# Expert tiles in pairs: two experts of 32 rows in four column quarters of the array, and a routing without the gain row and the GpSimd products

## What is computed

```python
def hier_moe(h, w_rg, b_rg, w_re, b_re, w_gate, w_up, w_down):
    g_logits = hf @ w_rg + b_rg                        # 4 groups
    g_idx = argmax(g_logits)
    e_in = (hf @ w_re + b_re)[the 8 experts of g_idx]
    top_v, top_i = lax.top_k(e_in, 2)
    combine = softmax weight of the group x softmax of top_v
    out = sum over experts: (silu(x @ w_gate) * (x @ w_up) * combine) @ w_down
x = x + hier_moe(rmsnorm_2(x, ffn_norm), ...)
```

## Time and the profile before

| | us |
|---|---|
| median of 3 runs | 1720.14 (1718.44 to 1720.27) |
| the profiled execution's own time | 1715.29 |
| its span, first to last instruction | 1713.6 |
| mean granted TensorE clock over the span | 0.983 |
| PE busy, PEld busy | 1629.1, 1308.2 |
| DVE, ACT, POOL busy | 938.9, 786.5, 193.6 |
| chain that ended last, share of PE | 82% |

### The profile page before, as it was taken

The page is one execution under the profiler, slowest core; times in us unless marked ns, Lnnn a source line. Parts: engine busy times, 40 slices in busy tenths (PEclk is TensorE's granted clock), DMA queues, the critical chain, the costliest instruction groups (busy, mean ns, idle before and its releaser), DMA issues.

```text
span 1713.6 us, 22648 instructions
## 1 busy us (share of the span) xinstructions
PE 1629.1 (95%) x9347; PEld 1308.2 (76%) x9347; DVE 938.9 (55%) x1347; ACT 786.5 (46%) x1261; POOL 193.6 (11%) x241
## 2 busy tenths in 40 slices
PE   7999999999999999988999989899999994999998
PEld 6888888788887888876788879879989884555554
DVE  5454677654565454577645465887858656111112
ACT  6434544543456444476644445557746531112121
POOL 0000000100010000011100010500001003343441
PEclk9999999999999999999999999999999995999999
DMA  7454555455565455531555544424432375999993
GB/s 283 174 195 174 194 185 192 164 189 180 192 222 206 181 192 177 195 124 70 189 174 195 175 154 172 148 74 167 164 136 101 151 302 203 347 410 403 407 408 152
DMA packets 58455, 347.94 MB, mean 203 GB/s; under 512 B 13629, under 2 KB 13917, under 8 KB 18129
## 3 DMA queue, kind: packets, MB, share of 16 engines
q1 hardware_dynamic: 47520, 334.02, 52.7%
q0 software_dynamic: 10832, 12.48, 2.3%
HBM read 372.57 MB, written 13.89 MB: 226 GB/s over the span
## 4 chain that ended last, share of the span: by engine, by line
PE 82%; DVE 9%; ACT 3%; issue 2%; DMA 2%; POOL 1%; SPq 0%; DVEq 0%; ACTq 0%; POOLq 0%
PE A L397 30%; PE Y L427 19%; PE A L2946 8%; PE A L350 5%; PE A L335 4%; PE Y L2964 4%; DVE wlo L295 2%; PE A L411 1%; PE Y L366 1%; ACT whi L290 1%; DMA raw<-stream 1%; PE A L694 1%; PE A L2937 1%; DVE xn L494 1%; DVE h L495 1%
## 5 line engine op out<-in xcount | busy, mean ns | idle before, releaser
L295 DVE TENSOR_TENSOR wlo<-raw,whi 128x2048 fp32r<-128x2048 f32 (+1 forms) x227 | 499.2, 2206 | 241.8 <-ACT whi L290 241.3
L290 ACT ACTIVATE whi<-raw 128x2048 fp32r<-128x2048 f32 (+1 forms) x227 | 417.7, 1847 | 89.9 <-DMA raw<-stream 89.6
L397 PE MATMUL A<-whi,xh 128*128 128x512 f32 x768 | 310.0, 404 | 5.3 <-DVE wlo L295 5.3
L397 PE MATMUL A<-wlo,xh 128*128 128x512 f32 x768 | 302.4, 394 | 0.0
L397 PE MATMUL A<-whi,xl 128*128 128x512 f32 x768 | 300.7, 391 | 0.0
L397 PEld LDWEIGHTS A<-whi,xh 128*128 128x128 f32 x768 | 145.0, 189 | 35.3 <-DVE wlo L295 6.1
L397 PEld LDWEIGHTS A<-whi,xl 128*128 128x128 f32 x768 | 145.2, 189 | 32.6
L397 PEld LDWEIGHTS A<-wlo,xh 128*128 128x128 f32 x768 | 145.4, 189 | 27.3
L427 PE MATMUL Y<-whi,hh 128*128 128x512 f32 x352 | 140.4, 399 | 1.2 <-DVE hl L774 1.2
L427 PE MATMUL Y<-whi,hl 128*128 128x512 f32 x352 | 139.2, 395 | 0.0
L427 PE MATMUL Y<-wlo,hh 128*128 128x512 f32 x352 | 139.1, 395 | 0.0
(11 more groups left out here) (461 smaller groups left out, 2873.6 us busy)
## 6 DMA issues: line engine op xcount, KB each, us to landing
raw<-stream SPq DMA_DIRECT2D x246, 1024.0 KB
far<-stream SPq DMA_DIRECT2D x28, 1024.0 KB
raw_whi<-stream SPq DMA_DIRECT2D x28, 1024.0 KB
raw_x<-stream SPq DMA_DIRECT2D x11, 1024.0 KB
gains<-post_rows POOLq DMA_DIRECT2D x6, 512.0 KB, 4.5
h<-x_in SPq DMA_DIRECT2D x2, 512.0 KB, 7.1
raw<-stream SPq DMA_DIRECT2D x4, 256.0 KB, 5.7
attn_bias<-attn_const POOLq DMA_DIRECT2D x1, 1024.0 KB, 7.1
```

The lines of the kernel that those rows point to most:

```text
L290: nc.scalar.activation(whi[:, n % RING, c], raw[:, n % RING, c], ACT.Copy).then_inc(hi_ready.sem, 1)
L295: nc.vector.tensor_tensor(wlo[:, n % RING, c], raw[:, n % RING, c], whi[:, n % RING, c].bitcast(F32), ALU.subtract).then_inc(lo_ready.sem, 1)
L397: ins = nc.tensor.matmul(bank, lhsT=lhs[:, kk, tok(t)], rhs=w[:, k, :], start=(kk == 0 and q == 0), stop=(kk == KD - 1 and q == 2))
```

## The change

- A tile holds 32 rows of one expert (`ROWS`), there are 16 extra tiles, and two tiles go together as a pair: 24 pairs, 16 of experts and 8 of extras. Each of the two experts has two quarters of 32 columns of the array, one for each of its two column blocks.
- The three pieces of weights of a pair are two slots each. The 19 places stay. The order of the pieces is as that of before, in pieces of two slots.
- The counts are compared with 7 multiples of 32 (`chunk`) instead of 3 of 64.
- The gain row, its load and the bias's load go. The bias is part of the constants. GpSimd's two products with the gain go: the raw h is stored in `rows_at` as soon as it is final, and the gain is multiplied in when the transposed rows are copied out of PSUM (`rows_copy`). The zero fill of `gx` is a transfer instead of a GpSimd instruction.
- The product that makes 128 ranks comes first in `Route.pe`, and its copy and the fill of `data` come before the logits' operations on VectorE. The running counts, the totals and the ranks are waited for one by one, and the counts are read in PSUM.
- Table products write one quarter of the array's columns each: 16 products per table, not 4.
- GpSimd scatters q - 1 before it issues an extra's weights (six transfers now, for q + 2).

```diff
-ROWS = 64
-EXTRA = 7
+ROWS = 32
+EXTRA = 16
+TIMES = 7
 TILES = EXPERTS + EXTRA
+PAIRS = TILES // 2
...
-def tiles_in_order():
+def pairs_in_order():
     order = []
-    for e in range(EXPERTS):
+    for e in range(EXPERTS // 2):
         order.append(e)
-        if e % 4 == 3 and e // 4 < EXTRA:
-            order.append(EXPERTS + e // 4)
+        if e in (2, 4, 6, 8, 10, 11, 12, 13):
+            order.append(EXPERTS // 2 + len(order) - e - 1)
     return order
...
             def pool(self, pool):
-                pool_rstd(pool, 0)
                 for t in range(NT):
                     pool.wait_ge(new_h[t].sem, self.free[t])
-                pool.dma_start(self.br[:, :], rows["route"].partition_broadcast(P)...)
-                pool.dma_start(self.gr[:, :], rows["moe"].partition_broadcast(P)...)
-                pool_rstd(pool, 1)
-                pool.wait_ge(route_in.sem, 32)
-                for t in range(NT):
-                    nc.gpsimd.tensor_tensor(xn[:, t, :], h[:, t, :], self.gr[:, :], ALU.mult).then_inc(scaled_in.sem, 1)
-                for t in range(NT):
-                    pool.wait_ge(scaled_in.sem, t + 1)
-                    pool.dma_start(rows_at[t * P:(t + 1) * P, :], xn[:, t, :]).then_inc(rows_out.sem, 16)
-                plink(pool, nc.gpsimd.memset(self.gx[:, :, :], 0.0))
+                    pool.dma_start(rows_at[t * P:(t + 1) * P, :], h[:, t, :]).then_inc(rows_out.sem, 16)
+                    if t:
+                        pool.dma_start(self.gx[:, :, :], nothing...[:, 0:3, 0:D // 2]).then_inc(nothing_in.sem, 16)
+                    pool_rstd(pool, t)
...
+                nc.tensor.matmul(Y[:, 1, 608:736], lhsT=ones, rhs=tri, start=True, stop=True).then_inc(counted.sem, 1)
                 pe.wait_ge(picked.sem, 1)
...
-                        ins = nc.tensor.matmul(at_[:, 0:4 * (b - a)], lhsT=self.in_tile[:, k, :],
-                                               rhs=self.entries[:, k, a:b, :]..., start=k == 0, stop=k == 2 * NT - 1)
+                        for g in range(4):
+                            ins = nc.tensor.matmul(at_[g * ROWS:(g + 1) * ROWS, 0:2 * (b - a)]...,
+                                                   lhsT=self.in_tile[:, k, :], rhs=self.entries[:, k, a + g % 2:b:2, :], ...)
...
-                dve.wait_ge(route_in.sem, 32)
+                dve.wait_ge(counted.sem, 1)
+                v.tensor_copy(self.ranks[:, :], Y[:, 1, 608:736])
+                (the six copies into data and the memset of sums, moved here from weights)
...
+            def chunk(self, dve, dst, n, width):
+                v = nc.vector
+                vlink(dve, v.tensor_tensor(self.past[:, 0:width, :], n.unsqueeze(2).broadcast_to([P, width, TIMES]),
+                                           cst[:, C_TIMES:C_TIMES + TIMES]..., ALU.is_gt))
+                vlink(dve, v.tensor_reduce(dst, self.past[:, 0:width, :], X, ALU.add))
...
                 for q in range(PAIRS):
                     if q + 3 < PAIRS:
                         gather(q + 3)
-                    if q + 4 < TILES and ORDER[q + 4] >= EXPERTS:
-                        weights(q + 4)
                     if 0 <= q - 1 < SENT:
                         scatter(q - 1)
+                    if q + 2 < PAIRS and ORDER[q + 2] >= EXPERTS // 2:
+                        weights(q + 2)
...
                     for k in range(4):
-                        for c in range(2):
-                            ins = nc.tensor.matmul(gate_up(q)[group(c), :], lhsT=xt[:, q % 2, k, group(part)], rhs=w[:, k, c, :], ...)
+                        for j in range(2):
+                            for c in range(2):
+                                ins = nc.tensor.matmul(gate_up(q)[group(c, j), :], lhsT=xt[:, q % 2, k, group(part, j)],
+                                                       rhs=w[j][:, k, c, :], ...)
...
-                    v.tensor_copy(xt[:, q % 2], rows_bank(q)...)
+                    v.tensor_tensor(xt[:, q % 2]..., rows_bank(q)..., gain.unsqueeze(3).broadcast_to([P, 4, 2, 2 * ROWS]), ALU.mult)
```

More of the change, by code:

```diff
@@ L2597, in build @@
         extras = 0
-        for m in range(3 * TILES):
-            q, part = PIECES[m]
-            if ORDER[q] < EXPERTS:
+        for m in range(6 * PAIRS):
+            q, part = PIECES[m // 2]
+            if ORDER[q] < EXPERTS // 2:
                 at = place_loaded[m % PLACES]
@@ L2604, in build @@
             else:
-                if part == 0:
-                    extras += 48
+                if part == 0 and m % 2 == 0:
+                    extras += 96
                 loaded.append((extra_loaded.sem, extras))
@@ L2613, in load_expert @@
         def load_expert(sp, m):
-            q, part = PIECES[m]
-            if ORDER[q] < EXPERTS:
+            q, part = PIECES[m // 2]
+            if ORDER[q] < EXPERTS // 2:
                 wait_place(sp, m)
-                sp.dma_start(places[m % PLACES], stream[first_static + 3 * ORDER[q] + part, :, :]
+                sp.dma_start(places[m % PLACES], stream[first_static + 3 * (2 * ORDER[q] + m % 2) + part, :, :]
                              ).then_inc(loaded[m][0], 16)
@@ L2639, in __init__ @@
                 self.sums = sb("sums", [P, 2, 48], where=where)
-                self.counts = sb("counts", [P, 224], where=where)
+                self.ranks = sb("ranks", [P, P], where=where)
                 self.over = sb("over", [P, NT, 32], where=where)
@@ L2801, in extras @@
                 full, sums, over, pw, pf, moved, xo = self.full, self.sums, self.over, self.pw, self.pf, self.moved, self.xo
-                total = self.counts[:, 64:96]
-                vlink(dve, v.tensor_scalar(full[:, :], total, float(ROWS), None, ALU.is_gt))
-                for c in (2, 3):
-                    vlink(dve, v.scalar_tensor_tensor(full[:, :], total, float(c * ROWS), full[:, :], ALU.is_gt, ALU.add))
+                total = A[:, 2, 0:32]
+                dve.wait_ge(counted.sem, 3)
+                self.chunk(dve, full[:, :], total, 32)
                 vlink(dve, v.tensor_copy(sums[:, 0, 16:48], full[:, :]))
@@ L2887, in _ @@
             def _(sp):
-                for m in range(2, 3 * TILES):
+                for m in range(2, 6 * PAIRS):
                     load_expert(sp, m)
@@ L2955, in down @@
                     wait_weights(pe, q, 2)
[L2956 removed]
+                    w = [weights_of(q, 2, j).rearrange("p (f c n) -> p f c n", f=2, c=2) for j in range(2)]
                     pe.wait_ge(expert_copied.sem, q + 1)
@@ L2977, in _ @@
                 turn_rows(0)
-                for q in range(TILES):
+                for q in range(PAIRS):
                     half(q, 0)
@@ L3050, in _ @@
                     for t in range(NT):
-                        ins = v.tensor_scalar(sel[:, i, tok(t)], choice.counts[:, 96:224], token[:, t, i:i + 1], None, ALU.is_equal)
+                        ins = v.tensor_scalar(sel[:, i, tok(t)], choice.ranks[:, :], token[:, t, i:i + 1], None, ALU.is_equal)
                 ins.then_inc(tail_ready.sem, 1)
-                for q in range(TILES):
-                    if q + 1 < TILES:
+                for q in range(PAIRS):
+                    if q + 1 < PAIRS:
                         rows_copy(q + 1)
```

165 lines of the change are left out of this document (83 added, 82 removed).

## The result

Measured 1740.24 us in the median of 4 runs (1737.34 to 1745.19), against 1720.2 for the kernel before on the same chip (1718.44 to 1720.5). The ratio is 1.012, with a 95% interval of 1.0098 to 1.0142: 1.2% slower, where 1697.5 us was forecast and slower had a chance of 0.12. The profiled execution took 1738.94 us, its span 1737.3, and the mean granted clock of TensorE fell from 0.983 to 0.952.

What follows compares the result with a forecast made beforehand. TensorE was taken to set the pace before, the weight stream after the change: loads from 1453.4 + 225 = 1678.4 us, read-back to 1683.8, sums 1686.8, then 5.3; span 1691, median 1697.5 us (-22.6), range 1686 to 1712.

Steps and rivals of the forecast that it cites:

- TensorE against DMA: Expert stage: TensorE needs 149 us plus 25 for eight empty pairs, 174 in all; the DMA's 225 us stream becomes the bound.
- Bytes and packets: Expert-stage transfers: the same 80 loads, stream unchanged at 225 us, GpSimd's 122 us hidden, scatters no longer on the path.
- quarters two at a time: Rival, expert products: four column quarters go no faster than two, 10.96 us per pair, median 1746 us; chance 7%.
- the clock: Rival, expert stage: TensorE waiting for weights drops to 1.2 GHz, 12.3 us per pair, median 1765 us if throughout; chance 5%.
- theory A: Posed for the follow-up runs: skipped transfers, issued late, land only behind queued loads; TensorE waits and the DMA runs dry.
- Stream of 225 us: Expert-stage weight loads: the slowest DMA engine's stream takes 225 us, from the first load after routing to the last bytes.
- the rival of the mean engine: Rival, weight loads: late DMA engines catch up, so the stream is 215.6 us, 9.4 less, median 1688 us; chance 13%.
- the 6.2 taken: Expert products: four quarters run at once and issue allows a half of 1.8 us and a pair of 6.2 us.
- rivals of issue: Rival, expert products: records issue no faster than 108 ns each, pairs of 9.25 us, median 1705 us; chance 10%.
- the signs that the prediction named for being wrong: Back-to-back TensorE with halves near 3.5 us; clock 0.5 with DMA pausing; loads of extras holding rows; first half no earlier.
- Routing: Before the expert stage: first half 5.4 us earlier, bounds nothing to -8; three slow VectorE operations give back 5.6 us.
- The end: After the stream ends at 1678.4 us: read-back queues behind the last loads, done at 1683.8, sums at 1686.8; span 1691.

Runs made afterwards that it cites:

- experiment 1: Kernel after without the 48 skipped transfers and TensorE's waits for them, three plain loads in their first places, empty pairs still computed: 1691.37 us.
- experiment 2: Kernel after with the four skipped transfers for a pair's halves issued at q + 3, the down product's two at q + 2 on their own semaphore: 1697.21 us.
- Experiment 3: Kernel before with an extra's three skipped transfers issued behind the scatter and at q + 2 instead of q + 4: 1781.83 us.
- experiment 5: Kernel after with the six skipped transfers issued ahead of the scatter, still at q + 2: 1711.62 us.
- experiment 7: Kernel after with SP's loads held to 13 slots ahead of TensorE instead of 19: 1755.9 us.
- experiment 6: Kernel after, same order and times of issue, with the down product's skipped transfers counted on a semaphore of their own: 1723.89 us.
- experiment 9: The kernel of experiment 2 with the down product's two skipped transfers moved ahead of the scatter: 1693.92 us.
- experiment 4: Kernel before with the routing half of the change alone, tiles and weights as before: 1715.06 us.
- experiment 8: Kernel after without skipped transfers and with the eight empty pairs not computed, 16 pairs left: 1677.58 us.

## Why the prediction was wrong

**The step that failed** is in "TensorE against DMA": "eight empty pairs with twice the skipped transfers. If each costs two of today's gaps, 25 us". They cost 114 us of waiting (107 and 7) and 15 us of lower clock. Its root is in "Bytes and packets": "Scatters now go before the weights of an extra; they are not on the path any more." The scatter is not, but what is queued behind it is. I costed GpSimd's 122 us as a share of 225 (hidden), and never placed the six transfers in time: they are issued at q + 2, not q + 4, behind a wait for the pair's output. The step from q + 4 tiles to q + 2 pairs looks the same when counted in experts, but only the first has slack. Experiments 1, 2 and 3 show it from three sides: without the transfers -49 us, issued early -43, and the kernel before with late issue +61. The chance of 0.12 for slower came from two rivals, quarters two at a time and the clock; neither was the cause, and the one that was stood among no rivals.

**Why a skipped transfer takes long: it takes turns with the loads.** The pages count the packets of GpSimd's queue (q0, packets, MB, share), of the kernel after and of experiment 1:

```profile
q0 software_dynamic: 12352, 12.63, 2.4%
...
q0 software_dynamic: 5440, 12.60, 2.1%
```

48 skipped transfers make 6912 packets, 144 each, and 0.03 MB: packets of 4 bytes. (Experiment 1 has three loads more and 432 packets more on SP's queue, so a load of 1 MB is 144 packets as well.) The kernel after from 1473 to 1483, and the kernel before from 1496 to 1499, by queue (q1 carries the loads):

```profile
q1 hardware_dynamic: 567, 4.12, 99.5%
q0 software_dynamic: 567, 0.00, 3.4%
...
q1 hardware_dynamic: 168, 1.23, 99.1%
q0 software_dynamic: 168, 0.00, 3.4%
```

The two queues move packet for packet: for each packet of 4 bytes one of the loads' passes, and those are mostly 8 KB. At 56.7 packets per us, 144 take 2.5 us and the six of a pair 15.2 us, an estimate from these rows; in experiment 5 the six landings of the second empty pair are 2.6 us apart. Where the loads stop, the packets hurry: 367 of them in the one us from 1649, with the sixth empty pair. That may be why the last landing and the end of the loads so often fell together, and it fits that the short queue of experiment 7 did not shorten the waits (286 packets of each queue from 1473 to 1478). That a skipped transfer does not stand behind the queued loads, experiment 5 shows. The last one of its second empty pair (chain), and a load that was issued 0.4 us before it, at 1495.65 (time from issue to landing):

```profile
1496.02 15.62 DMA raw<-stream,extra
...
DMA to landing us min/median/max: 21.6/21.6/21.6
```

It landed at 1511.6, that load at 1517.3. So theory A was right on the late issue and wrong on the queue. This is read from the traces; no run changed the number of packets alone. Experiment 3 has three skipped transfers where after has six, and its longest wait is 9.8 us, that of after 18.9. The Trainium skill (DMA: Bandwidth & Descriptors, Queues, rings and completion order) says that the increment of a semaphore is a strongly ordered write, which lands only after every earlier write of the same DMA engine, across its queues. That rule does not give the wait: in experiment 5 two loads issued earlier landed later, and no run here isolates what it adds.

**What the trace of before could have told.** TensorE waits nowhere for an extra's transfer there, since they went out four tiles, 24 us, ahead. So I put the landing at nothing and gave it no bounds. But the row above (168 packets against 168) stood there, and by it, with 144 packets for a transfer, six need about 15 us beside a full stream of loads, where two pairs, less the wait for the output, leave under 12. Measured from issue to landing: 2.1 to 21.2 us.

**Stream of 225 us.** Mis-sized: with nothing in the way it took 214 us (experiment 1), so the rival of the mean engine was the right one. The ragged end in the earlier trace rows came from places that TensorE freed late, not from slow engines' own backlog; that is argued from experiment 1, whose rate is 396 to 419 until 1660, not measured by engine. The end is ragged there too (299 to 193 GB/s from 1662 to 1668).

**TensorE.** Right: 1.73 us for a half of 32 records, 54 ns each, 6.0 us for a pair against the 6.2 taken. The Trainium skill (TensorE: Matmul & The Clock Gate, Part 3, measured speedup) gives 2.38 times for three column tiles; here four quarters do twice the products of two halves in the same 1.73 us, so for column quarters with 256 columns the measurement decides against a loss. The rivals of issue and of two quarters at a time fall with it.

**The clock.** Of the signs that the prediction named for being wrong, one appeared in part: a low granted clock with the DMA pausing. It was not 0.5 through the stage but 0.65 to 0.92 in windows of 20 us. The clock did fall to 0.50 in each long wait, but as an effect: 15 us of the loss in after, and in experiment 1 nothing that shows, since the loads are the bound.

**Routing.** -8.1 us at the first half, against -5.4; at the edge of its bounds (nothing to -8). The three slow operations gave 5.6 us as forecast (6.13 to 0.54), the pass over counts 0.62 twice as taken (1.3), the table products 1.08 us instead of 2.3.

**The end.** Right in kind: in experiment 1 the read-back takes 8.58 us instead of 5.74, as it stands behind the last loads, and four additions follow instead of two. (In the prediction's sum 1678.4 and 5.74 are 1684.1, not 1683.8; its next term is right again.) Its span of 1688.5 compares with the 1691 of the prediction. In the kernel after, the stall of 15.5 us in the last empty pair comes so late that nothing can take it back.

## What to carry to other kernels

A transfer that fetches nothing still has packets, and beside a full stream of loads each takes its turn with one of theirs: count its packets, not its bytes, issue it by time, not by steps, and keep it out of the shadow of an instruction that waits for output. When a change puts more work into a step of the bound engine, or makes the step faster, every prefetch distance becomes shorter in microseconds if it is kept by the amount of work: here four tiles of 6 us became two pairs of 6 us. Go through them one by one. And a stage in which both resources are below their limit is to be read as a handover, with the chain naming what is passed: look for the moment when one starts as the other ends.

## What the runs showed of the hardware

- An indirect transfer with every entry out of bounds costs GpSimd 1.0 us and the next one follows 0.3 us later, as before, and landed 2.1 to 16.8 us after its issue (experiment 5), 3.4 to 14.8 (experiment 6), 7.9 to 14.4 (experiment 7), 8.1 to 21.2 (experiment 9).
- Such a transfer is 144 packets of 4 bytes, as many packets as a load of 1 MB (6912 for 48, after against experiment 1), and they pass one for one with the loads' packets of 8 KB: 567 against 567 in 10 us at 412 GB/s. The last of a group of six landed 5.7 us before a load that had been issued ahead of it (experiment 5).
- Four column quarters of the array with 32 columns each ran at once without loss, 16 f32 products of 256 columns in 1.73 us.
- 32 records of table products on four quarters took 1.08 us in all at a granted clock of 0.50, 34 ns a record, less than the 56 ns that I took for the limit of issue from the earlier trace rows.
- VectorE operations of 8 elements took 2.00 us beside GpSimd's products and 1.71 us beside its memset; without either, in the kernel after and in experiment 4, they took 0.17 us.
- A single core's DMA ran at 416 to 421 GB/s for 180 us (experiment 8, 1460 to 1640).
